# Attention of the first two mixers in units of one PSUM bank, with queries on partitions and one pass of scores; trailing means and zeroed key halves on GpSimd

## The reference

```python
def pool_mixer(u, w_pool, pool_scale):      # trailing means over 2, 4, 8, 16 tokens
    cs = jnp.cumsum(u.astype(jnp.float32), axis=1)
    ...
        diff = (cs_g - lagged) / count - u[..., lo:hi].astype(jnp.float32)
        outs.append(diff.astype(u.dtype) @ w_pool[g])

def pool_fox_mixer(h, w_in, b_forget, w_pool, pool_scale, w_out):   # 8 heads of 64
    ...
    cum_log_f = jnp.cumsum(log_f, axis=1)
    y_fox = blocked_attention(q, k, v, FOX_HEAD_DIM ** -0.5, 1, cum_log_f)

def mla_mixer(h, cos, sin, ...):            # 16 heads, queries and keys of 96, values of 64
    ...
    y = blocked_attention(qk, k, v, (MLA_NOPE + MLA_ROPE) ** -0.5, CHUNK)

def blocked_attention(q, k, v, scale, chunk, log_decay=None):
    ...
        logits = jnp.einsum('bqhd,bkhd->bhqk', q_blk, k)
        logits = logits + (args[2][..., None] - fk[:, :, None, :])   # first mixer only
        p = jax.nn.softmax(jnp.where(allowed, logits, -jnp.inf), axis=-1)
        return jnp.einsum('bhqk,bkhd->bqhd', p, v)
```

## Time and profile before

| | |
|---|---|
| median of 3 runs | 2260.65 us (2240.28, 2260.65, 2261.16) |
| the profiled execution | 2260.9 us, of which the span of the trace is 2258.6 us |
| busy: PE, PEld | 2148.5 us (95%), 1767.7 us (78%) |
| busy: DVE, ACT, POOL | 1192.6 us (53%), 1010.4 us (45%), 42.0 us (2%) |
| mean granted clock of TensorE | 0.949 of full |
| first mixer's attention | 272.08 to 337.93 us |
| second mixer's attention | 787.4 to 875.8 us |

### The profile page before, as it was taken

How to read it: one execution, slowest core, us unless ns; L and a number is a source line. 1 busy time by engine, 2 the same in 40 slices (tenths; PEclk the granted TensorE clock), 3 DMA queues, 4 the chain that set the end, 5 groups by cost and what they waited for, 6 DMA issues and landing times.

```text
span 2258.6 us, 26535 instructions
## 1 busy us (share of the span) xinstructions
PE 2148.5 (95%) x10114; PEld 1767.7 (78%) x10114; DVE 1192.6 (53%) x1787; ACT 1010.4 (45%) x1571; POOL 42.0 (2%) x55
## 2 busy tenths in 40 slices
PE   7999999999999799999999997899977999799999
PEld 5888868888888687888788795788866888698887
DVE  5555516555655523655655542655446554586554
ACT  5444415444444523544544443544355443465443
POOL 1000000000000000000000000000000000200000
PEclk9999959999999878999999996999997999899999
DMA  9553504545654302656455352265425654303551
GB/s 313 178 172 115 198 0 154 201 167 166 214 178 151 112 19 64 206 169 203 146 204 172 112 180 100 85 214 174 160 75 183 209 179 156 112 1 127 190 199 42
DMA packets 239913, 338.92 MB, mean 150 GB/s; under 512 B 5495, under 2 KB 205342, under 8 KB 239694
## 3 DMA queue, kind: packets, MB, share of 16 engines
q1 hardware_dynamic: 239134, 336.15, 44.0%
q0 software_dynamic: 496, 1.23, 0.2%
q10 hardware_dynamic: 192, 0.30, 0.0%
HBM read 336.61 MB, written 1.05 MB: 149 GB/s over the span
## 4 chain that ended last, share of the span: by engine, by line
PE 92%; DVE 4%; ACT 2%; POOL 1%; issue 1%; DMA 0%; SPq 0%; ACTq 0%; DVEq 0%; POOLq 0%
PE A L489 10%; PE A L491 10%; PE A L490 10%; PE G L489 9%; PE G L491 8%; PE G L490 8%; PE X L489 7%; PE X L491 7%; PE X L490 7%; PE X L955 2%; PE G L955 1%; DVE wl L485 1%; PE G L790 1%; PE A L1331 1%; POOL st L673 1%
## 5 line engine op out<-in xcount | busy, mean ns | idle before, releaser
L485 DVE TENSOR_TENSOR wl<-raw,wh 128x1024 fp32r<-128x1024 f32 x557 | 656.4, 1218 | 238.7 <-ACT wh L476 238.1
L476 ACT ACTIVATE wh<-raw 128x1024 fp32r<-128x1024 f32 x557 | 563.1, 1056 | 150.0 <-PE A L491 139.5
L489 PE MATMUL G<-wh,xh 128*128 128x512 f32 x768 | 306.4, 399 | 14.4 <-DVE xl L1973 14.4
L491 PE MATMUL G<-wh,xl 128*128 128x512 f32 x768 | 301.5, 393 | 0.0
L490 PE MATMUL G<-wl,xh 128*128 128x512 f32 x768 | 301.4, 392 | 0.0
L489 PE MATMUL X<-wh,xh 128*128 128x512 f32 x656 | 259.4, 395 | 0.0
L491 PE MATMUL X<-wh,xl 128*128 128x512 f32 x656 | 255.8, 390 | 0.0
L490 PE MATMUL X<-wl,xh 128*128 128x512 f32 x656 | 255.5, 389 | 0.0
L489 PEld LDWEIGHTS G<-wh,xh 128*128 128x128 f32 x768 | 145.6, 190 | 44.6 <-issue 15.4
L491 PEld LDWEIGHTS G<-wh,xl 128*128 128x128 f32 x768 | 145.4, 189 | 31.5
L490 PEld LDWEIGHTS G<-wl,xh 128*128 128x128 f32 x768 | 145.7, 190 | 29.0
(11 more groups left out here) (420 smaller groups left out, 3062.6 us busy)
## 6 DMA issues: line engine op xcount, KB each, us to landing
raw<-in_ffn_w_in SPq DMA_DIRECT2D x88, 1024.0 KB, 6.1
raw<-in_ffn_w_gate SPq DMA_DIRECT2D x44, 1024.0 KB, 5.5
raw<-in_ffn_w_up SPq DMA_DIRECT2D x44, 1024.0 KB, 7.5
raw<-in_ffn_w_down SPq DMA_DIRECT2D x44, 1024.0 KB, 6.3
raw<-in_ffn_w_out SPq DMA_DIRECT2D x44, 1024.0 KB, 7.0
raw<-in_a_w_in SPq DMA_DIRECT2D x12, 1024.0 KB, 6.8
raw<-in_ab_w_in SPq DMA_DIRECT2D x8, 1024.0 KB, 7.3
raw<-in_kv_w SPq DMA_DIRECT2D x6, 1024.0 KB, 6.1
```

Of the source, the lines that this page charges most:

```text
L476: nc.scalar.activation(hi, r, ACT.Copy).then_inc(hi_done[u], 1)
L485: nc.vector.tensor_tensor(lo, r, hi.bitcast(F32), ALU.subtract).then_inc(lo_done[u], 1)
L489: nc.tensor.matmul(o, sh, rh, start=start, stop=False)
L491: return nc.tensor.matmul(o, sl, rh, start=False, stop=stop)
```

## The change

Both attentions take the NSA mixer's form. A unit is one bank. Of three units, which together serve four heads, two have the later 128 queries against 256 keys for two heads each (two lanes), and one has the earlier 128 queries against 128 keys for all four (four lanes). That is 12 units in the first mixer and 24 in the second. Queries and keys are split into a high and a low part, and each lane's scores are three fp32r matmuls in place of one fp32 product; the second pass of scores, the turned maxima and `keep_clock` are gone; four transposes and one ACT copy for each unit are new. The gate matmul now uses all 128 rows, on a tile `xh[:, 0, :]` that is zeroed outside the gates' rows.

```diff
+            def whole_mask(name, t):
+                at = 2 * P if t else 3 * P
+                block = masks_r[name][:, at:at + (t + 1) * P]
+                return block.unsqueeze(1).to_broadcast([P, 4 // (t + 1), (t + 1) * P])
+            def turn(name, n):
+                pe.wait_ge(unit_e, BASE[name] + n + 1)
+                for i in range(4):
+                    last = nc.tensor.transpose(X[n % 2][:, i * P:(i + 1) * P], probs[:, n % 2, i * P:(i + 1) * P], ident)
+                last.then_inc(unit_t, 1)
...
+            def scores3(name, n, mask, pairs, rows_of=None):
+                t, heads = unit_of(name, n)
+                if n >= 2:
+                    pe.wait_ge(unit_e, BASE[name] + n - 1)
+                w = (t + 1) * P
+                mm(G[n % 2][:, :].rearrange("p (l s) -> p l s", s=w), ident_r, whole_mask(mask, t), start=True, stop=False)
+                for l, h_ in enumerate(heads):
+                    o = G[n % 2][:, l * w:(l + 1) * w]
+                    if rows_of:
+                        mm(o, pick_r[:, h_:h_ + 1].to_broadcast([P, P]), rows_of[:, 0:w], start=False, stop=False)
+                    qh, ql, kh, kl = pairs(h_)
+                    at = slice(t * P, (t + 1) * P)
+                    last = mm3(o, qh[:, at], ql[:, at], kh[:, 0:w], kl[:, 0:w], False, l == len(heads) - 1)
+                last.then_inc(unit_s, 1)
```

The order on PE in the first mixer, and in the second the turning of heads ahead of the scores:

```diff
+                for n in range(-2, UNITS["fox"] + 1):
+                    if n + 2 < UNITS["fox"]:
+                        scores3("fox", n + 2, "causal", pairs, xh[:, 0, :])
+                    if 0 <= n < UNITS["fox"]:
+                        turn("fox", n)
+                    if n >= 1:
+                        values("fox", n - 1, lambda heads, l: fox["v"][:, :, heads[l], :])
...
+                turn_heads(0, 4)
+                for n in range(-2, UNITS["mla"] + 1):
+                    if n + 2 < UNITS["mla"]:
+                        if n % 3 == 1:
+                            pe.wait_ge(qk_lo, 4 * ((n + 2) // 3) + 4)
+                        scores3("mla", n + 2, "chunk64", pairs)
+                    turn_heads(*MLA_TURNS(n))
```

The trailing means move to GpSimd, which also makes the zeroed halves of the keys, four products of 128x1024 by a column of ones and zeros:

```diff
+            def low_keys():
+                G_ = nc.gpsimd
+                def halves(part, whole):
+                    for odd in range(2):
+                        last = G_.tensor_scalar(part[odd], whole, cst("halves")[:, odd:odd + 1], None, ALU.mult)
+                    return last
+                pool.wait_ge(event("fox_qk_lo"), 8)
+                halves(fox["k"][0], fox["k_hi"].bitcast(F32))
+                wait_rows(pool, "fox")
+                G_.tensor_scalar(xh[:, 0, :], tri, 0.0, None, ALU.mult).then_inc(event("fox_rows_zero"), 1)
+                halves(fox["k"][1], fox["k_rest"]).then_inc(event("fox_k_lo"), 1)
```

```diff
-                small(1, "fox_f", A[3], lambda i: A[2][:, 8 * i:8 * i + 8]).then_inc(small_done, 1)
+                    if i == 0:
+                        small_turn(1, "fox_f", lambda t: A[2][:, 8 * t:8 * t + 8]).then_inc(small_done, 1)
+                pe.wait_ge(event("fox_logf"), 1)
+                running_sums(fox["logf"].rearrange("p (t n) -> p t n", t=NT), None, A[3], event("fox_sums"))
                 for g in range(4):
-                    pe.wait_ge(tlin_out, tl[0] - 3 + g)
...
+                pe.wait_ge(event("fox_k_lo"), 1)
```

## The result

The changed kernel takes 2161.57 us, the median of 4 runs (2160.85 to 2165.81), against 2260.9 us before: a ratio of **0.9585** (95% interval 0.9529 to 0.9641). The forecast was 2215, with a range of 2198 to 2243. The sign and the mechanism were right; the gain is about twice as large as forecast, and the time lies outside the range. The profiled execution took 2160.85 us. Executions of the kernel before spread over 23 us in all (2238.44 to 2261.85), those of the changed kernel over 5, so medians are compared with medians, and stages by their marks in the traces. The start of a stage shifts by up to 1 us from one trace to the next, so a stage's length is taken from its own first scores.

The account below looks back on a forecast made before the run. PE alone, by its work and its clock, was taken to bound both attentions. First mixer -30.0, second -11.5, behind them -4.4: -45.9 from 2260.9 us gives 2215 us (-2.0%), range 2198 to 2243.

Parts of the forecast that it names:

- rival C: Both attentions: PE stays at half clock throughout, so the kernel gets slower, 2311 us; chance 0.08.
- Price of a unit: PE time at full clock, two and four lanes: 2.52 and 3.35 us first mixer, 2.28 and 2.90 second.
- Number of units: Two-lane and four-lane units: eight and four in the first mixer (33.6 us), sixteen and eight in the second (59.7).
- A: The forecast itself: clock above 0.9 in both attentions, 2215 us, own range 2200 to 2229; chance 0.55.
- B: Both attentions at a clock of 0.7 to 0.9; at 0.8, 2235 us; chance 0.2.
- Start of the first attention: First mixer: attention begins at 270.6 us instead of 272.08, 1.5 us earlier, set by DVE's last low part.
- rival D: GpSimd late in the first mixer: at 5 ns a column attention starts at 277, 2225 us; chance 0.03.
- Start of the second: Second mixer: first scores at 792.7 instead of 788.74, 5.3 us after the first turned head at 787.4.
- 3 us of waits in the second mixer: Added because ACT and DVE each serve exponents, heads and copies in one order: 3 us.
- Rival E: Second mixer: ACT and DVE set the pace, 3.5 us a unit, 2229 us in all; chance 0.09.
- -4.4 us behind the attentions: The 3.67 and 5.20 us after each attention, at clock 0.51 before, take half at full clock: -4.4 us.
- "Nothing" in the stages behind: Later stages, PE bound at clock 1.00, were forecast to change by nothing despite less idle time for weight transfers.

Follow-up runs that it names:

- The 40-row kernel: Changed kernel with the first mixer's gate matmul back to weights of 40 rows instead of 128: 2181.71 us (ratio 0.9684).
- the fillers: Changed kernel with 16 unused matmuls of 512 columns on PE in the wait ahead of each of the two attentions: 2166.02 us (ratio 0.9616).
- doubled scores: Changed kernel with the matmuls of every unit's scores (mask, gates, products) issued twice into the same bank: 2184.35 us (ratio 0.9677).

## Why the prediction was right or wrong

- **PE and its clock bound both attentions: right**, and shown by widening the weights alone. The weight load "that nothing covers" beside the fp32 product went with the narrow weights: the fp32 products that stayed repeat without it. The prediction named these weights in its weighing of rival C, but did not price what removing them alone would bring.
- **Price of a unit: right** to 0.02 us in four of four (2.52, 3.35, 2.29, 2.88). The values of 0.112 and 0.12 us for a matmul came from rows of another mixer.
- **Number of units: wrong by a factor of two.** "Eight and four units" and "Sixteen and eight units" should be four and two, eight and four. The units were counted as if three of them served two heads, and not four as the text on the change says; the turning of heads, 12 x 0.43, was counted rightly. This is the failed step: 16.8 + 29.9 = 46.7 us.
- **The clock: right**, A over B and C. From the first scores on, the mean clock is 0.91 in the first and 0.93 in the second. The spells at half rate were put at 2 us each: the first costs 0.8, as the fillers showed, and in the second 5.28 us at 0.50 lose 2.6. Rival C fell with the count as well. At half rate throughout, 51.8 us of PE work would be 103.6, against 147.0 of the old spans, so even that kernel would have been faster (2218 us by the same sum); its 0.08 for "slower" rested on the doubled work. The 40-row kernel shows it: half clock in the first attention, and still 26 us ahead of the old kernel there.
- **Start of the first attention: wrong by 1.5 us.** Forecast 270.6, measured 272.06. DVE's last low part did end at 270.6, as forecast (269.76 + 0.87); PE then waited for GpSimd's low keys, which ended at 272.0. A product by a column of ones and zeros took 2.84 us on GpSimd, 2.8 ns a column, where the copy's 1.2 was taken. The prediction had put the end of the cover at 2.2 ns: past it, so rival D is true in its mechanism, at a price of 1.4 us and not 10.
- **Start of the second:** 5.3 us forecast between the first turned head and the first scores, 6.1 measured; DVE's two splits of weights (738.67 to 741.0) stood ahead of its first low part.
- **3 us of waits in the second mixer:** PE idles 38.89 - 37.98 = 0.9 us there, from its first scores on. Rival E is out by the same number: at 33.61 us for the rest of the stage PE is busy 32.70, and with doubled scores 13.9 of 14.8 us of new work show.
- **-4.4 us behind the attentions:** -1.7 and -1.6, 1.1 us less.
- **"Nothing" in the stages behind: wrong by 5.7 us** in the profiled pair, the mLSTM's clock. I had not looked whether an unchanged stage's clock repeats from one trace to the next.

With the count right, the terms left were off by +2.0 (second mixer), -1.1 (behind the attentions) and +5.7 (mLSTM), and 0.3 came at the end: 6.9 in all, which takes 2168.3 to 2161.4, measured 2161.6. The first mixer's terms cancel: +1.4 in its length, -1.5 in its start.

## What to carry to other kernels

Price one unit from rows, but take the number of units from the code and test it against a second count, here heads turned or masks issued: this forecast had each price right to 0.02 us and missed by 53 us, 47 of them by the count. Where PE is busy at half clock, look at the rows of its weights and at idle time of the loader ("issue") before rewriting the stage; widening them with zeros gave about two thirds of the gain of a full rewrite here. GpSimd is dear for plain products (2.84 us where DVE takes 0.75), and a stage whose clock differs from trace to trace hides what small edits elsewhere are worth. Before a stage is compared between two traces, look where it begins in each.

## What the runs showed of the hardware that was not expected

- In the first mixer's new attention, gate weights of 40 or 64 rows among full ones went with a clock of 0.50 to 0.51 with PE 98% busy, and (shown at 40 rows) loader gaps of 0.22 us and more around them; with 96 rows neither is there (19.38 us against 39.72 for the same stage). In the mLSTM mixer the clock reached 1.00 with 40-row weights still among the others, but only 7 to 31 us after its attention began, against 3 to 6 with 128 rows.
- GpSimd took longer for a product by one column or by a constant (2.84 us for 1024 columns, written as fp32r, and 0.85 for 256) than for the sum of two tiles of 1024 (1.89); DVE took 0.75 for the same product. Side by side both slow down: 3.65 us on GpSimd, and 5.68 instead of 3.49 for three splits on DVE.
